# State-space rounds of a transformer pair: one 32-row matmul in place of two, on one Trainium2 core

## What is computed

```python
def segsum(a):
    t = a.shape[-1]
    cs = jnp.cumsum(a, axis=-1)
    diff = cs[..., :, None] - cs[..., None, :]
    mask = jnp.tril(jnp.ones((t, t), dtype=bool))
    return jnp.where(mask, diff, -jnp.inf)

def ssd_chunked(xdt, a, bm, cm):
...
    CB = jnp.einsum("bclgn,bcsgn->bgcls", Cc, Bc)
    M = CB[:, :, None] * jnp.exp(segsum(A))
    y_diag = jnp.einsum("bgrcls,bcsgrp->bclgrp", M, X)
    decay_states = jnp.exp(A_cs[..., -1:] - A_cs)
    states = jnp.einsum("bclgn,bgrcl,bclgrp->cbgrpn", Bc, decay_states, X)
...
    y_off = jnp.einsum("bclgn,cbgrpn,bgrcl->bclgrp", Cc, prev, jnp.exp(A_cs))
    return (y_diag + y_off).reshape(b, s, h, p)
```

## Time and profile before

| | |
|---|---|
| median of 3 runs | 925.79 us (925.61 to 929.63) |
| profiled execution, whole | 920.72 us |
| its span, first to last instruction | 918.9 us |
| PE busy | 894.4 us (97%) |
| DVE busy | 668.6 us (73%) |
| ACT busy | 512.5 us (56%) |
| POOL busy | 79.0 us (9%) |
| DMA | 168.00 MB, mean 183 GB/s |
| granted TensorE clock, mean | 0.994 |

### The profile page before, as it was taken

One profiled execution on the slowest core, in us unless ns is written; L12 is line 12 of the kernel. 1 busy time (PEld: TensorE's weight loads), 2 busy tenths in 40 slices (PEclk: granted clock), 3 DMA queues, 4 the chain that ended last, 5 costly groups with the idle time before them and its releaser, 6 DMA issues.

```text
span 918.9 us, 18092 instructions
## 1 busy us (share of the span) xinstructions
PE 894.4 (97%) x7444; PEld 851.2 (93%) x7444; DVE 668.6 (73%) x918; ACT 512.5 (56%) x696; POOL 79.0 (9%) x56
## 2 busy tenths in 40 slices
PE   5999999999999999999999999999998999999998
PEld 3899998888888889999999999988998999999998
DVE  6877998998699988777866545545886766666642
ACT  2566756577878774335555543446567654554431
POOL 0133000000455440000000000000000000000000
PEclk9999999999999999997999999999999999999999
DMA  9764553757322237483755655544431345555660
GB/s 377 305 244 147 198 190 121 280 217 251 116 90 93 92 131 260 184 302 118 283 191 183 206 206 184 183 155 167 139 138 47 138 144 200 206 184 183 231 205 23
DMA packets 25084, 168.00 MB, mean 183 GB/s; under 512 B 2868, under 2 KB 4532, under 8 KB 5048
## 3 DMA queue, kind: packets, MB, share of 16 engines
q1 hardware_dynamic: 23760, 164.90, 50.7%
q10 hardware_dynamic: 1256, 2.12, 0.7%
HBM read 165.95 MB, written 1.06 MB: 182 GB/s over the span
## 4 chain that ended last, share of the span: by engine, by line
PE 75%; DVE 10%; ACT 7%; DMA 4%; issue 3%; SPq 0%; DVEq 0%; ACTq 0%
PE bank L1864 74%; DVE wlo L1107 3%; ACT whi L573 3%; DMA raw<-w_stream 2%; DVE acc L1152 1%; DMA adas<-w_stream 1%; DVE cvt L1341 1%; ACT kw__113 L822 1%; PE bank L2137 1%; DVE eb L1432 1%; ACT ew L789 0%; DVE p L1319 0%; ACT prob L724 0%; PE bank L2161 0%; DVE kw__113 L1441 0%
## 5 line engine op out<-in xcount | busy, mean ns | idle before, releaser
L1864 PE MATMUL bank<-hhi,whi 128*128 128x256 f32 (+1 forms) x1364 | 382.8, 283 | 0.9 <-DVE hlo L1210 0.6
L1864 PE MATMUL bank<-hlo,whi 128*128 128x256 f32 (+1 forms) x1352 | 375.4, 278 | 0.0
L1864 PE MATMUL bank<-hhi,wlo 128*128 128x256 f32 (+1 forms) x1352 | 373.7, 278 | 0.0
L1107 DVE TENSOR_TENSOR wlo<-raw,whi 128x2048 fp32r<-128x2048 f32 (+1 forms) x130 | 298.9, 2300 | 101.0 <-ACT whi L573 98.9
L573 ACT ACTIVATE whi<-raw 128x2048 fp32r<-128x2048 f32 (+1 forms) x132 | 250.9, 1901 | 97.2 <-PE bank L1864 71.9
L1864 PEld LDWEIGHTS bank<-hhi,whi 128*128 128x128 f32 (+1 forms) x1364 | 256.0, 188 | 10.8 <-issue 9.9
L1864 PEld LDWEIGHTS bank<-hlo,whi 128*128 128x128 f32 (+1 forms) x1352 | 255.4, 189 | 0.2
L1864 PEld LDWEIGHTS bank<-hhi,wlo 128*128 128x128 f32 (+1 forms) x1352 | 253.7, 188 | 0.0
L1864 PE MATMUL bank<-fhi,whi 128*128 128x256 f32 x432 | 119.2, 276 | 0.0
L1864 PE MATMUL bank<-flo,whi 128*128 128x256 f32 x432 | 119.2, 276 | 0.0
L1864 PE MATMUL bank<-fhi,wlo 128*128 128x256 f32 x432 | 119.2, 276 | 0.0
(11 more groups left out here) (298 smaller groups left out, 1320.1 us busy)
## 6 DMA issues: line engine op xcount, KB each, us to landing
raw<-w_stream SPq DMA_DIRECT2D x147, 1024.0 KB, 4.9
adas<-w_stream SPq DMA_DIRECT2D x8, 1024.0 KB, 8.7
xres<-x_t SPq DMA_DIRECT2D x1, 1024.0 KB, 10.2
out<-oute SPq DMA_DIRECT2D x8, 128.0 KB, 4.1
tabs<-tabs_in_dram ACTq DMA_DIRECT2D x1, 641.0 KB, 8.7
tabs<-tabs_in_dram ACTq DMA_DIRECT2D x1, 512.0 KB, 3.6
hankel<-bucket_rows ACTq DMA_DIRECT2D x1, 512.0 KB, 10.8
cols<-cols_in_dram ACTq DMA_DIRECT2D x1, 325.0 KB, 8.2
```

The costliest lines, as they stand in the source:

```text
L1107: nc.vector.tensor_tensor(out=wlo[:, c % RING, 0:n], in0=raw[:, r % RING, 0:n], in1=whi[:, c % RING, 0:n].bitcast(f32), op=ALU.subtract)\
L1864: return nc.tensor.matmul(out, lhsT, rhs, start=start, stop=stop)
```

## The change

The running sums are laid out so that the 32 rows of a group are neighbours: eight heads, four roles (two parts by two). Each (t, d) has its own 128 columns of `csr`. POOL makes from it `css`, in which the roles differ (`row_roles`, two instructions), so that one 32-row matmul gives both terms of the exponent: `decays` has two matmuls where it had four. POOL also adds the even and odd slots of `bd` (`pair_rows(t)`, once for each token chunk), and one 32-row matmul with the fixed weight `par` replaces the two with `grp`; `group_halves` is gone. The two masks are applied in one DVE instruction. `csr`, `css` and `pairs_` lie in the memory of `xres`, so x is loaded a second time (1 MB), on ACT's queue, and `tabs2` is issued beside it, earlier than before.

```diff
+            def row_roles():
+
+                nc.gpsimd.tensor_scalar(css[:, :, :], csr[:, :, :].bitcast(f32), marks[:, 0, 1:2], marks[:, 1, 0:1],
+                                        ALU.mult, ALU.add).then_inc(csr_done, 1)
+                pool.wait_ge(csr_done, 3)
+                nc.gpsimd.tensor_scalar(csr[:, :, :], csr[:, :, :].bitcast(f32), marks[:, 0, 0:1], marks[:, 0, 1:2],
+                                        ALU.mult, ALU.add).then_inc(csr_done, 1)
+
+            def pair_rows(t):
+
+                d = 1 - t
+                own = bd[:, d * HG:(d + 1) * HG, :].bitcast(f32).rearrange("p (j two) l -> p two j l", two=2)
+                if t == 1:
+                    pool.wait_ge(bc_done, NG)
+                pool.wait_ge(bd_done, 2 + 2 * t)
+                nc.gpsimd.tensor_tensor(out=pairs_[:, :, :], in0=own[:, 0], in1=own[:, 1], op=ALU.add)\
+                  .then_inc(bd_done, 1)
...
             for i in range(8):
-                group_halves(i)
                 if i == NG:
                     pool.wait_ge(segb_done, NG)
                     own_rows(1, 1)
...
                     if i == NG - 1:
                         pool.wait_ge(segf_done, NG)
                         own_rows(1, 0)
+                        pair_rows(1)
                     squares(i - 2)
...
+                if k == 11:
+                    act.wait_ge(yd_done, 8)
+                    act.dma_start(tabs2[:, :], tabs2_dram).then_inc(tabs2_in, 16)
+                    act.dma_start(xres[:, :, :], x_dram).then_inc(x_in, 16)
             split(FIRST["so"] + AHEAD)
...
-                if i == 0:
-                    act.wait_ge(yd_done, 8)
-                    act.dma_start(tabs2[:, :], tabs2_dram).then_inc(tabs2_in, 16)
...
-                for dst, mask in ((cbf, "le"), (cbb, "ge")):
-                    nc.vector.tensor_tensor(out=dst[:, :], in0=side[2][:, 0:P], in1=tab(mask),
-                                            op=ALU.mult).then_inc(cbm_done, 1)
+                masks = tabs[:, TSPAN["le"][0]:TSPAN["ge"][1]].rearrange("p (a l) -> p a l", a=2)
+                nc.vector.tensor_tensor(out=cb2[:, :, :], in0=spread(side[2][:, 0:P], 1, 2), in1=masks,
+                                        op=ALU.mult).then_inc(cbm_done, 1)
...
             dve.wait_ge(mod_done, 3)
+            dve.wait_ge(x_in, 32)
...
-                pe.wait_ge(bd_done, 2 * t + 2 - t)
-                pe.wait_ge(grp_done, i + 1)
-                for part in range(2):
-                    own = bd[:, (1 - t) * HG:(2 - t) * HG, :].rearrange("p (j two) l -> p two j l", two=2)[:, part]
-                    last = mm(side[4][:, :], grp[:, i % 2, HD - part * HD:HD - part * HD + P], own, part == 0, part == 1)
-                last.then_inc(bc_done, 1)
...
+                pe.wait_ge(bd_done, 3 + 2 * t)
+                rows = slice(g * 4 * HG, (g + 1) * 4 * HG)
+                mm(side[4][:, :], par[rows, :], pairs_[rows, :, :]).then_inc(bc_done, 1)
...
                 for k in range(2):
-                    heads = d * NH + g * HG + 4 * k
-                    mm(side[k][:, :], group(g, P), bd[:, d * HG + 4 * k:d * HG + 4 * k + 4, :], True, False)
-                    last = mm(side[k][:, :], csr[:, t, :], spread(ind[:, heads:heads + 4], 2, P), False, True)
+                    last = mm(side[k][:, :], css[rows, 2 * t + d, :], bd[rows, d * HG + 4 * k:d * HG + 4 * k + 4, :])
```

111 lines of the change are left out of this document (53 added, 58 removed).

## The result

Sixteen runs of each kernel: the changed kernel took 928.72 us in the median (925.25 to 935.85), the kernel before 926.44 us (923.81 to 929.63). The ratio is 1.0038, with a 95% interval of 1.0019 to 1.0056. So the change costs about 3.5 us, 0.4%, where I forecast a gain of 0.5 us. The time of 928.72 us is still inside the range (921.6 to 928.8 us), by 0.1 us and by luck, since it holds about 2 us that the runs could not place; the case within 0.5% had 0.75, but the middle has the wrong sign.

A forecast was written before the change was run, and what follows sets the result against it. PE sets the pace up to 264 us, then DVE and POOL, which exclude each other. The start's +0.4 is contained in 0 at 281.58, then -0.5, loads 0: 925.79 - 0.5 = 925.3 us; range 921.6 to 928.8 us.

The forecast's parts named there:

- the case within 0.5%: Whole kernel: the changed time differs from the one before by no more than about 0.5%, 4.6 us; chance 0.75.
- PE: PE in the rounds: ten matmuls of 0.22 us become five, saving 1.1 us in a round, 8.8 us in all.
- Rival 4: 32-row matmuls save PE almost nothing, 0.15 us in a round, their 0.19 us loads not hidden: 925.7 us; chance 0.06.
- Before the rounds: POOL's `row_roles` holds DVE's `smax` scaling, 0.6 us; the merged subtraction gives back 0.2 us: net +0.4 us.
- Rounds 0 to 2: PE saves 1.1 us in each and DVE follows, so `eb` of round 2 starts 2.4 us earlier.
- Rounds 2 to 3: The gain is lost where POOL's `own_rows` and `pair_rows(1)` block DVE's `kw_` group and `sslo`.
- 0 at 281.58: DVE's `kw_` at 281.58 us: middle taken between about 0.8 us later and 0.6 to 0.9 us earlier.
- Rounds 4 to 7: DVE and POOL set the pace; merged mask instruction and dropped casts save 0.5 us together, bounds -0.3 and -1.2 us.
- The loads: x and `tabs2` loads at the end of the rounds, beside the chunk loads: 0, bounds 0 and +3.8 us.
- rival 3: Reload of x hits the weight stream; PE's wait for `rcol` comes up to 3.8 us later: 929.1 us alone; chance 0.10.

The follow-up runs named there:

- a_rows128: Changed kernel with its five 32-row matmuls of a round over all 128 rows, only its time being read: 1.0024 of the kernel before, rounds 93.64 us.
- a_ideal: Changed kernel with pairs made before the rounds, x reloaded inside them, `tabs2` at its old place, five matmuls over 128 rows: 1.0040 of the kernel before.
- a_wait: Changed kernel in which POOL's `own_rows(1, 1)` waits until DVE's `sslo` of round 1 is done: 1.0040 of the kernel before, rounds 92.47 us.
- a_mixload: `a_mix0` with both loads (`tabs2` and all of x) back where the change has them, behind round 7: 0.9986 of the kernel before.
- a_mix0: `a_mix` with `dsel2` at the end of the memory, so that no other buffer moves: 0.9967 of the kernel before.
- a_early: Changed kernel with x reloaded in two parts inside the rounds and `tabs2` at its old place: 1.0049 of the kernel before, rounds 93.98 us.
- a_mix: `a_wait` with x reloaded inside the rounds, `tabs2` at its old place, second block's pairs in one product after round 2's `xd`: 1.0066 of the kernel before.

## Why the prediction was wrong

**PE (mis-sized, 8.8 us forecast, 1.4 us measured).** This is the first step that failed. I took 0.22 us for each of the five matmuls that were saved, and 128-row matmuls were all that my rows had. The matmuls themselves cost that (0.24 us), but each switch between 32 and 128 rows costs about 0.2 us, and a round has four: 1.1 - 0.78 leaves 0.3 us, measured 0.23. Rival 4 had this size (0.15 us in a round), but charged every 32-row matmul for it, not the switches. Its time of 925.7 us was still wrong, since it left POOL's part out.

**Before the rounds (wrong sign, small).** I expected +0.4 us from `smax` held behind POOL. It wasn't held, and the stage is 0.4 us shorter.

**Rounds 0 to 2 (follows from PE).** `eb` of round 2 was to come 2.4 us earlier, the loss at the start included. From the start of the rounds the `kw_` group of round 2 is 264.20 - 237.84 = 26.36 us away against 26.89 us: 0.5 us earlier, 0.9 us with the 0.4 us of the start.

**Rounds 2 to 3 (meetings right, result mis-sized).** This is the step that turned the sign. The `kw_` group took 4.61 us (4 or more forecast), `sslo` 2.38 us (over 2). That `own_rows(1, 0)` came at 266.73 us (forecast 266.6) is luck: it was to come 3.3 us earlier and comes 28.89 us after the start of the rounds against 29.55 us, 0.7 us earlier; the rest is xbc, 2 us shorter in this profile, and the start. In the second profile it stands at 270.33 us. I added the meetings to "0 at 281.58", the middle between two orders. Between the two groups 2.05 us were lost, and the group of 281.58 is 42.69 us after the start of the rounds against 41.17 us: +1.5 us. This step fails even with PE's saving: in `a_rows128` the group comes 282.30 - 239.48 = 42.82 us after the start, about 1 us of it for the clock, and in `a_ideal`, where `pair_rows(1)` is gone too and the clock stays, 41.24 us. So the 2.4 us that I let run into this place came through it in neither profile; and where `sslo` did get in first, as in `a_rows128`, the `kw_` group was longer and ACT late. `a_wait` shows that the order of `own_rows(1, 1)` and `sslo` alone is worth 1.5 us. With it restored the rounds are still 0.3 us slower than before, not faster.

**Rounds 4 to 7 (wrong sign, small).** Forecast -0.5 us; 331.92 - 280.53 = 51.39 against 51.00 us is +0.4. PE waits 3.4 us for `cb`, less than the 5 to 8 us forecast, because it saved less.

**The loads (taken at 0, open).** The place that I watched, `rcol` at 352 us, has no wait, so rival 3 as written is wrong. The loads do delay the next chunk by 2 to 5 us, around the 3.8 us that I priced, and PE's `so` chunk covers it, as I said. The place where the rest can show is 65 us later, behind `wo`: that PE waits there and loses its clock stood in the profile of before.

Of the 3.5 us, the rounds make 1.8 and the start -0.4. The other 2 us are not settled. "so, wo" is 95.42 and 93.92 us in the changed kernel and 92.80 and 94.23 us in the one before; `a_mixload` against `a_mix0` would put 2.9 us on the loads, the means over all profiles 0.5 to 0.7 us, and `a_early`, without them still at 94.17 us and 1.0049, speaks against more. With the interval of the ratio (1.0019 to 1.0056, 1.8 to 5.2 us) the 1.4 us of rounds and start fall short of the measured loss by 0.4 us at least.

## What to carry to other kernels

Count row-group switches, not only matmuls: five short ones that sit between 128-row work saved a sixth of what their number promised. Where DVE and POOL share the time, a gain upstream is worth only what can pass the next meeting of the two, so first ask which POOL instruction will wait when a long DVE one ends, and hold it back by one semaphore if the next DVE instruction is short and urgent. Keep the other buffers where they are when comparing two versions, compare stages before totals, and take more than one profile of each before a stage with waits and a falling clock is put down to the change.

## What I had not expected of the hardware

- Moving all buffers from `acc` on by 32 bytes makes PE's gemm stages 4.0 and 2.6 us longer, with no wait and a granted clock of 1.00: 509 instead of 532 matmuls in 60 us.
- A stage of gemms can also differ between two executions of the same kernel: 185.26 and 178.50 us, 1191 and 1238 matmuls in 140 us, both at a granted clock of 1.00.
- Waits of PE of 1.3 to 2.1 us behind `wo` were followed by stretches of 4 us at 0.50 to 0.70 of the clock, in `a_mix` a wait of 0.65 us too (0.84 and 0.50); with waits of 0.2 us the clock stayed at 1.00. In the rounds of the changed kernel, waits of 1.15 and 1.50 us left it at 1.00, and in `a_rows128` one of 3.49 us was followed by 0.67.
- A 32-row matmul costs 0.24 us behind its like and about 0.2 us more wherever it meets a 128-row one.
